# A hybrid mixer with an expert layer, in front of a retention and a stick-breaking layer: new step counts in the mixer, a conv read from PSUM, a first half pick, a new load order

## The reference

```python
def first_block(x, meta_tokens, ...):            # 16 meta rows ahead of 256 tokens: 272 rows
    h = concatenate([meta, x], axis=1)
    hn = rmsnorm(h, ln_mix_w)
    h = h + hybrid_mixer(hn, ...)                # below
    h = h[:, N_META:]
    hn = rmsnorm(h, ln_ffn_w)
    h = h + peer_ffn(hn, w_q, sub_keys, u_tab, v_tab)
    return rmsnorm(h, ln_final_w)

def hybrid_mixer(hn, ...):
    q, k, v, g_out, g_low, z, xbc, dt_raw, gate_a, gate_b = split_cols(hn @ w_in, IN_SPLITS)
    o = gla_chunked(q, k, v, log_g)              # 4 heads of gated linear attention
    y_a = (rmsnorm(o) * silu(g_out)) @ w_up_gla
    xbc = silu(causal_dwconv(xbc, conv_w, conv_b))   # 4 taps along the tokens
    xs, Bm, Cm = split_cols(xbc, ...)
    y = ssd_chunked(xs * dt, a, Bm, Cm) + d_skip * xs    # 4 groups of 8 heads
    y_b = rmsnorm(y * silu(z)) @ w_up_ssd
    return (sigmoid(gate_a) * y_a + sigmoid(gate_b) * y_b) @ w_out

def peer_ffn(h, ...):                            # per token and each of 8 heads
    s_top, i_top = top_k(scores, 16)             # for both halves of the key
    best, pos = top_k(all 256 sums, 16)          # 16 experts of 16384
    u = u_tab[idx]; act = gelu(u . h)
    out = sum(softmax(best) * act * v_tab[idx])
```

## Time and profile before

| | us |
|---|---|
| median of 3 runs | 1598.37 (1596.96 to 1599.61) |
| the profiled execution | 1598.98 |
| its span, first to last instruction | 1597.1 |
| PE busy in the span | 1390.8 (87%) |
| DVE busy | 1086.7 (68%) |
| ACT busy | 735.5 (46%) |
| POOL busy | 297.6 (19%) |

### The profile page before, as it was taken

The page is one execution under the profiler, slowest core; times in us unless marked ns, Lnnn a source line. Parts: engine busy times, 40 slices in busy tenths (PEclk is TensorE's granted clock), DMA queues, the critical chain, the costliest instruction groups (busy, mean ns, idle before and its releaser), DMA issues. The chain is left out here.

```text
span 1597.1 us, 19058 instructions
## 1 busy us (share of the span) xinstructions
PE 1390.8 (87%) x6585; PEld 997.3 (62%) x6585; DVE 1086.7 (68%) x2077; ACT 735.5 (46%) x1270; POOL 297.6 (19%) x260
## 2 busy tenths in 40 slices
PE   6998978899999788877877878678799999999997
PEld 6987978787989433333333333233398688998776
DVE  5767467875668777777777777675687466765664
ACT  5665777747455322222222222221354466656772
POOL 0000000000003555444544445443100000000000
PEclk9999989999999899898989889999999999999999
DMA  6353444444567999999999999999755456454542
GB/s 227 125 181 87 152 133 132 146 132 156 176 206 299 420 421 420 422 421 421 421 422 421 422 420 422 421 421 421 309 176 173 132 173 196 152 176 135 151 138 81
DMA packets 77808, 417.73 MB, mean 262 GB/s; under 512 B 8768, under 2 KB 8832, under 8 KB 44688
## 3 DMA queue, kind: packets, MB, share of 16 engines
q0 software_dynamic: 36864, 268.45, 40.4%
q1 hardware_dynamic: 40848, 148.06, 29.1%
HBM read 415.39 MB, written 1.08 MB: 261 GB/s over the span
## 5 line engine op out<-in xcount | busy, mean ns | idle before, releaser
L321 PE MATMUL ps<-AR 128*128 128x512 f32 (+6 forms) x1164 | 362.0, 462 | 94.1 <-ACT AR L1213 68.0
L222 DVE TENSOR_TENSOR wlo<-raw,whi 128x1024 fp32r<-128x1024 f32 x257 | 311.6, 1221 | 154.1 <-ACT whi L221 153.4
L321 PEld LDWEIGHTS ps<-AR 128*128 128x128 f32 (+2 forms) x1164 | 190.1, 196 | 257.5 <-issue 127.5
L221 ACT ACTIVATE whi<-raw 128x1024 fp32r<-128x1024 f32 x257 | 269.3, 1054 | 121.3 <-PE ps L260 99.6
L321 PE MATMUL ps<-SLAB,AR 128*128 128x512 f32 x516 | 258.0, 656 | 62.8 <-ACT AR L1213 62.6
L260 PE MATMUL ps<-XH,whi 128*128 128x256 f32 (+1 forms) x1032 | 306.4, 297 | 4.7 <-DVE XL L332 2.4
L260 PE MATMUL ps<-XL,whi 128*128 128x256 f32 (+1 forms) x1032 | 296.7, 288 | 0.0
L260 PE MATMUL ps<-XH,wlo 128*128 128x256 f32 (+1 forms) x1032 | 296.6, 287 | 0.0
L1178 POOL DMA_INDIRECT AR<-in_peer_uv,C x127 | 151.6, 1194 | 654.6 <-DVE C L1132 487.9
L321 PEld LDWEIGHTS ps<-SLAB,AR 128*128 128x128 f32 x516 | 105.2, 208 | 211.0 <-issue 126.3
L260 PEld LDWEIGHTS ps<-XH,whi 128*128 128x128 f32 x1032 | 200.4, 194 | 13.5 <-DVE XL L332 5.5
(11 more groups left out here) (253 smaller groups left out, 1237.7 us busy)
## 6 DMA issues: line engine op xcount, KB each, us to landing
raw<-in_stream SPq DMA_DIRECT2D x257, 512.0 KB, 3.7
AR<-scr SPq DMA_DIRECT2D x8, 512.0 KB, 5.1
SLAB<-in_peer_uv,C POOLq DMA_INDIRECT x129, 28.1
AR<-in_rows SPq DMA_DIRECT2D x4, 512.0 KB, 4.7
AR<-in_peer_uv,C POOLq DMA_INDIRECT x127, 27.4
AR<-in_con SPq DMA_DIRECT2D x1, 1280.0 KB, 7.1
AR<-in_xin SPq DMA_DIRECT2D x2, 512.0 KB, 5.0
AR<-in_xin SPq DMA_DIRECT2D x1, 1024.0 KB, 8.0
```

The costliest lines, as they stand in the source:

```text
L221: a = A(lambda e: e.activation(h[:, :], r, ACT.Copy), loaded[i], free, chain=False)
L222: b = V(lambda e: e.tensor_tensor(l[:, :], r, h[:, :].bitcast(F32), ALU.subtract), a, loaded[i], free, chain=False)
L321: return PE(lambda e: e.matmul(out_ap, l, r, start=start, stop=stop, skip_group_check=onto), *after, signal=sig)
```

## The change

- Start: GpSimd clears the meta tile, x rows 128 to 255 are loaded ahead of the meta rows, which have a semaphore of their own; GpSimd scales the meta rows.
- `stream_T` runs a third side step after the sixth k tile when `ring["steps"]` is 3 (`stream_N` had such a third step before). The steps go to 3 with the fourth x tile (chunk 45) and back to 2 at `mix_side`, ahead of `w_up_ssd`.
- Empty steps are added: `gla_side` two before `attention(0)`, one before the first `features`, one before the second; `ssd_side` three at the start, two after `turn(1)`, two before the first output, one within each output; `y_side` waits four steps for each group.
- Conv: ACT's copy and XP are gone. The DVE instructions read the product in PSUM, with shifted columns, and the bank is free after the last of them.
- Expert layer: for the first `topk`, the first eight picks of the sums are turned into indices by themselves, six gathers are issued, then the other eight are picked and the rows weighted.
- Groups of one pick from m = 248.

```diff
+                            if k == 5:
+                                side_step(3)
...
-        z0 = V(lambda e: e.memset(HX[:, 2, :], 0.0))
+        m0 = G(lambda e: e.memset(HX[:, 2, :], 0.0))
         x0_in = dma(SP, HX[:, 0, :], x_tiles[:, 0, :], s_x)
-        x1_in = dma(SP, HX[0:16, 2, :], meta, s_x1, z0)
         x1_in = dma(SP, HX[:, 1, :], x_tiles[:, 1, :], s_x1)
+        meta_in = dma(SP, HX[0:16, 2, :], meta, s_m, m0)
...
-                V(lambda e, f=f: e.tensor_scalar(HX[0:16, 2, f], HX[0:16, 2, f], ss[0:16, 2:3], None, ALU.mult))
+                g = G(lambda e, f=f: e.tensor_scalar(HX[0:16, 2, f], HX[0:16, 2, f], ss[0:16, 2:3], None, ALU.mult), r)
...
-                ready = (ready[1], (v, a)) if c else (None, (v, a))
+                ready = (ready[1], (v, a, g)) if c else (None, (v, a, g))
...
             def use(o, tok):
-                p = f % 2
-                a = A(lambda e: e.copy(XP[:, p, 3:3 + T], o), tok, xp_free[p], v0)
                 w = P_CONVW + 4 * f
-                a = d = A(lambda e: e.activation(dst, o, ACT.Identity, bias=par_(P_CONVB + f), scale=par_(w + 3)), first_free())
+                d = A(lambda e: e.activation(dst, o, ACT.Identity, bias=par_(P_CONVB + f), scale=par_(w + 3)), tok, first_free())
                 for j in range(3):
-                    v = V(lambda e, j=j: e.scalar_tensor_tensor(dst, XP[:, p, j:j + T], par_(w + j), dst, ALU.mult, ALU.add), d)
-                xp_free[p] = v
+                    late_by = 3 - j
+                    v = V(lambda e, j=j, n=late_by: e.scalar_tensor_tensor(dst[:, n:T], o[:, 0:T - n], par_(w + j), dst[:, n:T],
+                                                                           ALU.mult, ALU.add), d)
                 silu()
                 late.append((f, dst, v))
-                return a
+                return v
...
                 if f % 4 == 3:
+                    ring["steps"] = 3
                     sides.append(ssd_side(f // 4))
...
-            for _ in range(4 if g == 3 else 2):
+            for _ in range(4):
                 yield
...
         pts["z_done"] = PE.now()
+        until("yT7")
...
+            if n == 0:
+                V(lambda e: e.max(BV[:, 0:8], CAND))
+                V(lambda e: e.max_index(idx[:, 0:8], BV[:, 0:8], CAND))
+                early["idx"] = pairs(slice(0, 8))
+                yield
+                V(lambda e: e.match_replace(CAND, BV[:, 0:8], CAND, NEG))
+                V(lambda e: e.max(BV[:, 8:16], CAND))
+                V(lambda e: e.max_index(idx[:, 8:16], BV[:, 8:16], CAND))
+                v = V(lambda e: e.tensor_scalar(SM[:, 28:29], BV[:, 0:1], -1.0, None, ALU.mult))
+                idx_pt[n] = pairs(slice(8, 16))
...
-            for _ in range(3):
+            for _ in range(2):
                 next(first_topk)
-            weighted_rows()
...
+            for m_next in range(6):
+                gather(m_next)
+            m_next = 6
+            next(first_topk)
+            weighted_rows()
             gathers()
...
-                size = 4 if m < 228 else 2 if m < 254 else 1
+                size = 4 if m < 228 else 2 if m < 248 else 1
```

More of the change, by code:

```diff
@@ L378, in build @@
         a = A(lambda e: e.activation(junk[:, 0, :], HX[:, 0, :], ACT.Square, accum_out=ss[:, 0:1]), x0_in, z0)
[L379 removed]
+        a = A(lambda e: e.activation(junk[0:16, 0, :], HX[0:16, 2, :], ACT.Square, accum_out=ss[0:16, 2:3]), meta_in)
         V(lambda e: e.tensor_tensor_reduce(junk[:, 1, :], HX[:, 1, :], HX[:, 1, :], 1.0, 0.0, ALU.mult, ALU.add, ss[:, 1:2]), x1_in)
@@ L687, in build @@
         CT = place("CT", 23312, 4 * T).rearrange("p (g t) -> p g t", g=4)
-        XP = place("XP", 24400, 552).rearrange("p (b t) -> p b t", b=2)
         XSG = place("XSG", 24952, 2176).rearrange("p (b f t) -> p b f t", b=2, f=4)
@@ L785, in ssd_side @@
             Mg = M[:, g % 2, :, :, :]
-            yield
-            yield
+            for _ in range(5):
+                yield
             silu()
@@ L970, in build @@
         sides.append(mix_side())
+        ring["steps"] = 2
         stream_T([(0, TX, cons_yb(f)) for f in range(8)], y_at, TX, yt_ready)
@@ L1102, in build @@
         iota16 = C1[:, C_IOTA:C_IOTA + 16]
-        idx_pt, w_pt, c_pt = {}, {}, {}
+        idx_pt, w_pt, c_pt, early = {}, {}, {}, {}
         def best16(vals, idx, src):
@@ new lines, in topk @@
+            idx = BI.bitcast(U32)
+            if n == 0:
+                V(lambda e: e.max(BV[:, 0:8], CAND))
+                V(lambda e: e.max_index(idx[:, 0:8], BV[:, 0:8], CAND))
+                early["idx"] = pairs(slice(0, 8))
+                yield
+                V(lambda e: e.match_replace(CAND, BV[:, 0:8], CAND, NEG))
[3 more added lines that the diff above has]
+                idx_pt[n] = pairs(slice(8, 16))
+            else:
+                best16(BV, idx, CAND)
+                v = V(lambda e: e.tensor_scalar(SM[:, 28:29], BV[:, 0:1], -1.0, None, ALU.mult))
+                yield
+                idx_pt[n] = pairs(slice(0, 16))
@@ L1152, in slot_free @@
                 return read.get(holds[j])
+            if j == 6 and "hn" not in pts:
+                return None
             if j < EARLY:
@@ L1178, in gather @@
             G(lambda e: e.indirect_dma_start(slots[j], None, peer_uv, bass.IndirectOffsetOnAxis(ap=col, axis=0)).then_inc(s, 16),
-              idx_pt[m // 16], free, signal=False, chain=False)
+              early["idx"] if m < 8 else idx_pt[m // 16], free, signal=False, chain=False)
             uv_in[m] = (s, dma_count[s.name])
```

35 lines of the change are left out of this document (18 added, 17 removed).

## The result

1586.88 us, the median of 4 runs (1586.06 to 1589.29), against 1597.89 (1596.96 to 1599.61) for the kernel before: ratio 0.9932, 95% interval 0.9915 to 0.9950. The change makes the kernel 11.0 us faster. The forecast was 26.3 us, to 1572: direction and range held, the size did not, and the range of the likeliest case by itself (1564 to 1581) was missed. The profiled execution of after has a span of 1585.2 us, 11.9 less than that of before.

The account below looks back on a forecast made before the run. PE, waiting for side work, was taken to bound the mixer and the DMA engines the expert layer. 1598.98 - 22.2 (mixer) - 2.6 (start) - 0 (gathers) - 1.5 (end) = 1572.7, stated as 1572 us, range 1560 to 1590.

Parts of the forecast that it names:

- Inside `ssd_side`: Mixer: state product and first output move further behind what they wait for, saving 0.5 and 1.0 us.
- New waits: Mixer: closer second outputs and turns may bring new PE waits, 0 to 8 us; 2.6 us lost taken.
- Clock: Mixer: PE's drops to 1.2 GHz at 132, 155 and 250 us go with their waits, saving 5.4 us.
- Conv: Mixer: DVE reading PSUM instead of SBUF costs nothing over 72 instructions; priced at 0.
- Length of the sides: Mixer: a group takes 8.3 chunks in place of 8, still ahead of what asks for it; priced at 0.
- Start: Kernel start: earlier x load brings the norm 2.0 us earlier, lighter DVE and ACT queues the rest; 2.6 us saved.
- First picks: Expert layer: gather 0 starts 2.4 us earlier, but an idle DMA gap before gather 17 eats the gain; 0.
- End: Expert layer's tail: single picks start with their own arrival, so PE ends earlier; 1.5 us saved, bounds 0 to 1.9.
- the waits travel along: Rival, mixer: ACT's load ahead of the silu moves with the turn, mixer gains only 9 us; 1585 us, chance 0.26.
- The banks bind: Rival, mixer's conv tiles: DVE lags beyond 9 us and PE waits for banks; slower, 1606 us, chance 0.07.
- the early start lasts: Rival, gathers: gather 17 is early too, so the 2.4 us are kept; 1570 us, chance 0.12.
- the start does nothing: Rival, kernel start: clearing on GpSimd takes 4 us or more; 1575 us, chance 0.05.

Follow-up runs that it names:

- later: The changed kernel with two more steps behind the first attention scores and five more ahead of group 1's state product: 1578.42 us, ratio 0.9873 to before.
- turn_undone: The changed kernel with group 1's silu and turn three steps earlier again (two steps ahead in place of five): 1583.68 us, ratio 0.9912 to before.
- picks_undone: The changed kernel with gather 0 after all sixteen picks again, as before: 1584.23 us, ratio 0.9909 to before.
- conv_sbuf: The changed kernel with the conv as before, ACT copying the tile out of PSUM and DVE reading the copy: 1590.77 us, ratio 0.9948 to before.
- start_undone: The changed kernel with the start as before (clearing and meta scalings on VectorE, meta rows loaded first): 1588.74 us, ratio 0.9948 to before.
- silu_later: The changed kernel with the silu of each conv tile one conv tile later in ACT's queue: 1585.72 us, ratio 0.9916 to before.
- table_pool: The changed kernel with the two products of each group's decay table on GpSimd instead of VectorE: 1585.83 us, ratio 0.9916 to before.
- best2: The changed kernel with more steps ahead of waiting readers, half of group 0's Abs on DVE, sixteen picks at once, meta scaling on DVE: 1577.87 us, 0.9884.

## Why the prediction was wrong

The direction held, and most terms with it. The step that failed is the pricing of the mixer "by how far its reader moves", in two terms: "Inside `ssd_side`", 1.5 saved, and "New waits", 2.6 lost; with it fell the term "Clock", 5.4 saved, which took the low stretches to go with their waits. The sign that the prediction named for being wrong, new waits inside `ssd_side` beyond 3 us, came.

- *Inside `ssd_side`*: the state product's wait rose from 1.2 to 5.5, the first output's fell from 3.2 to 1.7, L837 is new with 1.2: 4.0 lost for 1.5 saved. *New waits*: L641 alone 3.5, the price 2.6. Together 6.4 of the 8.9 us by which the mixer fell short. The step took each reader's own way as its gain and did not ask when DVE gets to the next one: DVE came to the masked scores only 0.5 us earlier while PE came 4.0 earlier, and L800 was reached at 288.64 us in after and at 288.69 in later, wherever PE stood. turn_undone shows a wait of group 2 set by what stands ahead of it in DVE's queue, with its own distance unchanged.
- *Attention(0)* 3.4 for 3.0, *silu* 10.2 for 11.0, *features* 2.3 for 3.0, *y_side* 1.6 for 0.9: right in sum (17.5 for 17.9). One of the two waits for features went whole, the other stayed at 2.4, so 3.0 was right only as a sum.
- *Clock*: 2.8 for 5.4, the other 2.6 of the shortfall. The stretches at 157, 249 and 368 us went with their waits, but the one at 133 came again at 136 behind the new wait for L641, one of 6.8 us came at 290 behind L800, and the one at 204 cost more than before (2.8 for 1.5), as PE waited less in it. The working priced every drop at 3.6 us; the one at 249 lasted 6.8, and the one at 211 had begun at 204, with PE waiting through most of it.
- What is left over is small: 0.9 gained at the first stream products, 0.2 lost in small waits.
- *Conv*, priced at 0: its instructions cost the same, as forecast; undoing it made the stage 5.7 us longer in one profile (2.3 of it waits), so it was worth some of the gain, through ACT's copies, which the step had counted only inside the silu's term. *Length of the sides*: nothing in the waits speaks against 0.
- *Start*: 1.64 for 2.6. The landing was right; the 0.6 from lighter queues and part of the norm's 2.0 were not there.
- *First picks*, 0 with bounds of 1.0 gained and 1.5 lost: 1.27 lost against before, 2.1 by picks_undone, 1.7 by the means above. Gather 0 came 2.8 us closer to the first query product (2.4 forecast). The gap that was forecast is there, but the larger one stands ahead of gather 9, whose slots wait for the query products; the working looked at gather 17 alone. Its delay of DVE by the double pair work, up to 1.4, is there with 1.1.
- *End*: 1.33 for 1.5, in the rows.
- Outside the working: 3.15 us of block two, about the cost of its two low stretches (1.7 us each, at 1160 and 1529 us). It hangs on the moment as much as on the program.

Of the rivals, "the waits travel along" (1585) came nearest, and that is luck: ACT's load did not move with the turn but began at the same time (189.47 and 189.45 us), the linear attention's gain went to L641, and group 1 kept its gain at the silu. "The banks bind", "the early start lasts" and "the start does nothing" fell (conv_sbuf, picks_undone, start_undone).

Still open: whether before meets the low clock in block two as often as after, what besides the Abs passes holds ACT at 200 us, what shortens the queue itself (silu_later and table_pool did little), and where the 4 us in best2 are.

## What to carry to other kernels

A wait for an in-order engine that is behind is not owned by its reader: price a moved reader by when that engine gets to the work, and look up who stands next in its queue, or the wait is only handed on. More steps paid once (later, 8.1 us of stage) and then no more (best2). Count the lower clock only where the engine was busy; where it waited, the wait has the time already. An earlier start of a transfer stage was worth nothing here, because a slot further on is released by work whose own loads then came later.

## What was not expected of the hardware

- The record has low stretches of 3.4 us, or two or three times that, and one of 3.4 us costs 1.7 us where PE is busy through it. The same block two, behind the same wait of 2.1 us (2.4 in conv_sbuf), meets one in some profiles and not in others (12 of 16). Two profiles of one kernel therefore differ by more than some of the parts measured here.
- GpSimd took 2.34 to 3.27 us for a product of 128x1024 (DVE 1.22), 0.91 to 1.08 for a scaling of 16x256 (0.34), and 0.95 for clearing 128x1024 (0.91).
